# Attention with half-height transposes, in the step order transposes, scores, values

## What is computed

```
s_c = q·kc * scale;      p_c = masked_softmax(s_c)     # compressed keys, 63 of them
s_s = q_rot·k_s * scale; p_s = masked_softmax(s_s)     # selected blocks
s_w = q_rot·k_w * scale; p_w = masked_softmax(s_w)     # window of 512
o = gates[..., 0:1] * (p_c @ vc) + gates[..., 1:2] * (p_s @ v_s) + gates[..., 2:3] * (p_w @ v_w)
```

## Time and profile before

| | |
|---|---|
| median of 3 runs | 2242.99 us (2241.25 to 2245.93) |
| profiled execution | 2246.47 us |
| its span | 2244.4 us |
| TensorE busy | 2174.4 us (97%) |
| VectorE busy | 948.7 us (42%) |
| ScalarE busy | 663.2 us (30%) |
| GpSimd busy | 456.7 us (20%) |
| mean granted TensorE clock | 0.989 |
| the attention loop | from about 181 to 448 us of the span |

### The profile page before, as it was taken

One profiled execution on the slowest core, in us unless ns is written; L12 is line 12 of the kernel. 1 busy time (PEld: TensorE's weight loads), 2 busy tenths in 40 slices (PEclk: granted clock), 3 DMA queues, 4 the chain that ended last, 5 costly groups with the idle time before them and its releaser, 6 DMA issues.

```text
span 2244.4 us, 28818 instructions
## 1 busy us (share of the span) xinstructions
PE 2174.4 (97%) x10100; PEld 1392.4 (62%) x10100; DVE 948.7 (42%) x2027; ACT 663.2 (30%) x1402; POOL 456.7 (20%) x890
## 2 busy tenths in 40 slices
PE   8998999999999999999999999999999999999996
PEld 6454665677678887888885556454544445454542
DVE  0226888764367785354444568411111111111114
ACT  2125666555425561111112220011111111111114
POOL 0002444301100000000000000134343434444340
PEclk9998999999999999999999999999999999999998
DMA  6302000065421111122213123699999999999955
GB/s 210 121 0 104 2 1 1 2 225 218 180 65 32 37 37 40 32 63 75 75 38 127 68 104 117 242 359 338 353 347 340 345 344 349 343 354 332 347 147 228
DMA packets 133213, 378.25 MB, mean 169 GB/s; under 512 B 23891, under 2 KB 81355, under 8 KB 105835
## 3 DMA queue, kind: packets, MB, share of 16 engines
q1 hardware_dynamic: 109587, 292.46, 35.1%
q0 software_dynamic: 23520, 84.36, 13.1%
HBM read 341.48 MB, written 58.00 MB: 178 GB/s over the span
## 4 chain that ended last, share of the span: by engine, by line
PE 87%; DVE 7%; ACT 3%; DMA 2%; issue 1%; SPq 0%; DVEq 0%; POOL 0%; ACTq 0%; POOLq 0%
PE PS L1458 20%; PE PS L1238 19%; PE PS L1469 10%; PE PS L765 9%; PE PS L878 5%; PE PS L1363 5%; PE PS L911 3%; PE PS L948 3%; PE PS L1053 2%; PE PS L813 2%; PE PS L1539 1%; PE PS L1402 1%; PE PS L1185 1%; PE PS L1347 1%; PE PS L1341 1%
## 5 line engine op out<-in xcount | busy, mean ns | idle before, releaser
L1238 PE MATMUL PS<-arena 128*128 128x258 f32 x2352 | 516.1, 382 | 6.3 <-DVE arena L2304 4.7
L1238 PEld LDWEIGHTS PS<-arena 128*128 128x128 f32 x2352 | 446.7, 190 | 73.9 <-DVE arena L2304 5.1
L1549 ACT ACTIVATE arena<-PS 128x512 f32<-128x512 f32 (+9 forms) x602 | 276.8, 471 | 707.3 <-PE PS L765 383.8
L1458 PE MATMUL PS<-arena 128*128 128x512 f32 x1040 | 457.2, 592 | 0.8 <-ACT arena L1549 0.8
L765 PEld LDWEIGHTS PS<-arena 128*128 128x128 f32 (+3 forms) x1950 | 236.6, 158 | 177.7 <-issue 121.4
L1458 PEld LDWEIGHTS PS<-arena 128*128 128x128 f32 x1040 | 192.9, 190 | 218.6 <-issue 217.6
L765 PE MATMUL PS<-arena 128*128 128x128 f32 (+3 forms) x1950 | 284.5, 277 | 25.3 <-DVE arena L2086 7.7
L1469 PE MATMUL PS<-arena 128*128 128x512 f32 x520 | 239.2, 593 | 0.5 <-ACT arena L1549 0.5
L2576 DVE TENSOR_TENSOR arena<-PS,arena 128x256 f32<-128x256 f32 x65 | 27.6, 425 | 432.2 <-ACT arena L1891 425.6
L1469 PEld LDWEIGHTS PS<-arena 128*128 128x128 f32 x520 | 94.0, 191 | 93.9 <-issue 93.3
L2680 POOL MEMSET arena<- 128x2 f32 x1 | 0.1, 100 | 747.4 <-PE PS L1363 747.4
(11 more groups left out here) (338 smaller groups left out, 2215.8 us busy)
## 6 DMA issues: line engine op xcount, KB each, us to landing
arena<-in_w_exp_gate SPq DMA_DIRECT2D x65, 1024.0 KB
arena<-in_w_exp_up SPq DMA_DIRECT2D x65, 1024.0 KB
arena<-in_w_exp_down SPq DMA_DIRECT2D x65, 1024.0 KB
arena<-in_w_in SPq DMA_DIRECT2D x34, 512.0 KB, 4.8
arena<-in_x_prompt SPq DMA_DIRECT2D x16, 512.0 KB, 5.1
expert_rows<-arena SPq DMA_DIRECT2D x16, 512.0 KB
arena<-expert_rows SPq DMA_DIRECT2D x6, 1024.0 KB, 11.0
arena<-in_w_in SPq DMA_DIRECT2D x16, 256.0 KB, 8.0
```

What stands on the lines that cost most here:

```text
L1238: ins = mm(PS[:, bank, 0:QT], lhs[:, l0 + k, :], right[:, r0 + k, c0:c0 + QT], start=first and k == 0, stop=k == kh - 1, skip_group_check= ...
L1458: ins = mm(PS[:, 2 + s, :].rearrange("p (h n) -> p h n", h=2), xgT[:, s, k, :], up_w[w][:, :, k, :], start=k == 0, stop=k == KT - 1)
L1549: return fn(out, in_, ACT.Copy)
```

## The change

`turn_probs` splits every 128x128 transpose into two: query rows 0 to 63 go to bank 4 and rows 64 to 127 to bank 5 (`turn_half`), for both heads, each from 64 partitions with 64 columns of the identity. It now waits for both copies of the unit before at its start. ScalarE copies the first half of the queries of both heads, VectorE the second half (`half_turned`); `PTs` keeps its layout. A compressed unit is copied by ScalarE alone, from both banks. TensorE's order at a place becomes transposes(k-6), scores(k), values(k-7). ScalarE does exps(k-1) and falls(k-1) at place k, after its copy; VectorE does its copy first, then maxima(k) and coefs(k-1). `coefs` leaves the gate out: in tiles 3 to 0 GpSimd's multiplication takes the gate and the reciprocal as its two scalars (the second was the constant 1.0); in tiles 7 to 4 GpSimd makes correction times gate once per group, in a small operation of its own that it waits for, and takes the reciprocal as second scalar. Epsilon moves to a buffer of its own, set in the mixing stage without a semaphore of its own.

```diff
--- before.py
+++ after.py
@@ -261,6 +261,12 @@
                 return kvraw[:, 5:9, P:2 * P].rearrange("p (g t) c -> p g t c", g=2)
             return at(TMP + (5632 if p == 3 else 2816 * half + 1024 * p), 2, u["n"], P)
 
+        def half_turned(k, h):
+
+            n = UNITS[k]["n"]
+            return (PTs[:, k % 2, :, 0:n * P].rearrange("p g (c h q) -> p g c h q", h=2, q=64)[:, :, :, h, :],
+                    PS[:, 4 + h, 0:n * P].rearrange("p (g c q) -> p g c q", g=2, q=64))
+
         def small(slot, off, *shape):
             n = int(np.prod(shape))
             assert off + n <= P
@@ -421,6 +427,7 @@
         widx = rowb[:, 0, 0:2]
         wrow = at(29700, 2)
         st4 = at(29664, 4, 8)
+        eps = at(29708, 1)
 
         met = [sem("pe_met"), sem("act_met"), sem("dve_met")]
 
@@ -765,6 +772,11 @@
                 return nc.tensor.transpose(out, in_, ident[0:n, 0:n])
 
 
+            def turn_half(out, in_, h):
+
+                return nc.tensor.transpose(out, in_[GP[h]], ident[GP[h], 64 * h:64 * h + 64])
+
+
             turned_into = []
 
             def next_bank():
@@ -917,18 +929,17 @@
                 pe.wait_ge(scale_done, k + 1)
                 if k:
                     pe.wait_ge(pt_ev[0], k)
+                if N_PT1[k] > (u["kind"] != "c"):
+                    pe.wait_ge(pt_ev[1], N_PT1[k] - (u["kind"] != "c"))
                 if u["kind"] == "c":
-                    for j in range(4):
-                        src = kvraw[:, 1 + 4 * (u["i"] % 2) + j, 0:P]
-                        ins = turn(PS[:, 4, j * P:(j + 1) * P], src, P)
-                    E.do(ins, pt_done)
+                    src = [kvraw[:, 1 + 4 * (u["i"] % 2) + j, 0:P] for j in range(4)]
                 else:
-                    for g in range(2):
-                        if g and N_PT1[k] > 1:
-                            pe.wait_ge(pt_ev[1], N_PT1[k] - 1)
-                        for c in range(u["n"]):
-                            ins = turn(PS[:, 4 + g, c * P:(c + 1) * P], probs(u)[:, g, c, :], P)
-                        E.do(ins, pt_done)
+                    src = [probs(u)[:, g, c, :] for g in range(2) for c in range(u["n"])]
+                for m, rows in enumerate(src):
+                    for h in range(2):
+                        ins = turn_half(PS[:, 4 + h, m * 64:(m + 1) * 64], rows, h)
+                        if m == len(src) - 1 and (h or u["kind"] != "c"):
+                            E.do(ins, pt_done)
 
             def values(k):
 
@@ -952,16 +963,16 @@
             for k in range(NU + LAG + 1):
                 if k == 2:
                     pe.wait_ge(tokT_ready, 3 * NT - 2)
+                if k == LAG:
+                    pe.wait_ge(tokT_ready, 3 * NT)
+                if 0 <= k - LAG < NU:
+                    turn_probs(k - LAG)
                 if k < NU:
                     scores(k)
                 if k == 0:
                     turn_tile(NT - 1, (2,))
                 if k == 4:
                     turn_tile(NT - 1, (0, 1))
-                if k == LAG:
-                    pe.wait_ge(tokT_ready, 3 * NT)
-                if 0 <= k - LAG < NU:
-                    turn_probs(k - LAG)
                 if 0 <= k - LAG - 1:
                     values(k - LAG - 1)
             E.arrive()
@@ -1655,16 +1666,18 @@
                     act.wait_ge(pt_done, N_PT[k - LAG] - (UNITS[k - LAG]["kind"] != "c"))
                     if k >= LAG + 2:
                         act.wait_ge(pv_done, k - LAG - 1)
-                    w = 512 if UNITS[k - LAG]["kind"] == "c" else UNITS[k - LAG]["n"] * P
-                    E.do(copy(PTs[:, (k - LAG) % 2, 0, 0:w], PS[:, 4, 0:w]), pt_ev[0])
+                    if UNITS[k - LAG]["kind"] == "c":
+                        E.do(copy(PTs[:, (k - LAG) % 2, 0, :].rearrange("p (j h q) -> p h j q", j=4, h=2), PS[:, 4:6, 0:256].rearrange("p h (j q) -> p h j q", j=4)), pt_ev[0])
+                    else:
+                        E.do(copy(*half_turned(k - LAG, 0)), pt_ev[0])
                 if k == 0:
                     tok_T(NT - 1, (2,))
                 if k == 4:
                     tok_T(NT - 1, (0, 1))
-                if k < NU:
-                    exps(k)
-                    if CHUNKED[k]:
-                        falls(k)
+                if 1 <= k <= NU:
+                    exps(k - 1)
+                    if CHUNKED[k - 1]:
+                        falls(k - 1)
             E.arrive()
 
 
@@ -1927,7 +1940,6 @@
                             with act.If(i * 2 + 1 < blocks):
                                 spare(i, 1)
 
-            act.wait_ge(sem("eps_set"), 1)
             for t in range(NT):
                 n = rows_of(t)
                 s, w = st4[0:n, t % 4, :], other[0:n, t, :]
@@ -1936,7 +1948,7 @@
                     act.wait_ge(sem("fin_done"), t - 3)
                 E.step(fn(w.rearrange("p (a b) -> p a b", a=2), PS[0:n, 2 * (t % 4):2 * (t % 4) + 2, :], ACT.Identity, scale=-1.0 / D, accum_out=s[:, 0:1]), sem("totalled"))
                 E.step(fn(w, w, ACT.Square, bias=s[:, 0:1], scale=-float(D), accum_out=s[:, 1:2]))
-                E.do(fn(s[:, 2:3], s[:, 1:2], ACT.Sqrt, bias=st4[0:n, 0, 7:8], scale=1.0 / D), sem("std_done"))
+                E.do(fn(s[:, 2:3], s[:, 1:2], ACT.Sqrt, bias=eps[0:n, :], scale=1.0 / D), sem("std_done"))
 
 
         @block.vector
@@ -2051,19 +2063,15 @@
                     E.do(tt(v, v, g4[:, 0], ALU.mult), coef_done)
                     return
                 h = u["group"] % 2
-                ga = g4[:, 1:3, :, u["j"]]
                 if u["group"] >= 2:
                     dve.wait_ge(scale_done, max(m for m in range(NU) if UNITS[m]["group"] == u["group"] - 2) + 1)
                 if i >= 4:
                     dve.wait_ge(fall_done, REL[k])
                     E.step(tt(part[:, h], fall[:, h], sums[:, h], ALU.mult))
                     E.step(tt(tot[:, h], part[:, h, :, 0, :], part[:, h, :, 1, :], ALU.add))
-                    E.step(V.reciprocal(tot[:, h], tot[:, h]))
-                    E.step(tt(tot[:, h], tot[:, h], ga, ALU.mult))
-                    E.do(tt(coef[:, h], fall[:, h], tot[:, h].unsqueeze(2).broadcast_to([P, 2, 2, 2]), ALU.mult), coef_done)
+                    E.do(V.reciprocal(tot[:, h], tot[:, h]), coef_done)
                 else:
-                    E.step(V.reciprocal(tot[:, h], sums[:, h, :, 0, :]))
-                    E.do(tt(coef[:, h, :, 0, :], tot[:, h], ga, ALU.mult), coef_done)
+                    E.do(V.reciprocal(tot[:, h], sums[:, h, :, 0, :]), coef_done)
 
             def block_out(i):
 
@@ -2071,19 +2079,18 @@
                 E.do(V.tensor_copy(AT[:, :, i * P:(i + 1) * P], PS[:, 6 + i % 2, :].rearrange("p (j q) -> p j q", j=4)), o_ev)
 
             for k in range(NU + LAG + 3):
+                if 0 <= k - LAG < NU and UNITS[k - LAG]["kind"] != "c":
+                    u = UNITS[k - LAG]
+                    dve.wait_ge(pt_done, N_PT[k - LAG])
+                    if k >= LAG + 2:
+                        dve.wait_ge(pv_done, k - LAG - 1)
+                    E.do(V.tensor_copy(*half_turned(k - LAG, 1)), pt_ev[1])
                 if k < NU:
                     maxima(k)
                 if k == 1:
                     rope_queries(NT - 1)
                 if 1 <= k <= NU and (UNITS[k - 1]["kind"] == "c" or UNITS[k - 1]["last"]):
                     coefs(k - 1)
-                if 0 <= k - LAG < NU and UNITS[k - LAG]["kind"] != "c":
-                    u = UNITS[k - LAG]
-                    dve.wait_ge(pt_done, N_PT[k - LAG])
-                    if k >= LAG + 2:
-                        dve.wait_ge(pv_done, k - LAG - 1)
-                    w = u["n"] * P
-                    E.do(V.tensor_copy(PTs[:, (k - LAG) % 2, 1, 0:w], PS[:, 5, 0:w]), pt_ev[1])
                 if 0 <= k - LAG - 2 < NU and (k - LAG - 1 == NU or UNITS[k - LAG - 1]["kind"] == "c"):
                     block_out(UNITS[k - LAG - 2]["i"])
 
@@ -2464,6 +2471,7 @@
                 dve.wait_ge(sem("mix_mm"), m + 1)
                 dve.wait_ge(s_xin[m % 2], 32 + 16 * (m // 2 + 1))
                 if m == 0:
+                    E.do(V.memset(eps[:, :], EPS))
                     dve.wait_ge(sem("mix_ev"), 1)
                     E.step(stt(y, xr[0:n, 0, :], ALPHA, y, ALU.mult, ALU.add), sem("xr_used"))
                 else:
@@ -2606,7 +2614,6 @@
                             with dve.If(i * 2 + 1 < blocks):
                                 spare(i, 1)
 
-            E.do(V.memset(st4[:, 0, 7:8], EPS), sem("eps_set"))
             for t in range(NT):
                 n = rows_of(t)
                 s, y = st4[0:n, t % 4, :], x1tok[0:n, t, :]
@@ -2637,9 +2644,14 @@
                     G.tensor_tensor(pc, pc, coefc[:, u["i"] % 2].unsqueeze(3).broadcast_to([P, 2, 4, 63]), ALU.mult).then_inc(scale_done, 1)
                 else:
                     h, kd = u["group"] % 2, "sw".index(u["kind"])
```

(7 more changed lines are left out.)

## The result

The changed kernel takes 2226.87 us (median of 4 runs, 2226.18 to 2227.41) against 2244.46 for the kernel before on the same chip: 17.6 us less by the medians. The ratio is 0.9916, 95% interval 0.9904 to 0.9928 (the medians alone give 0.9922, which lies inside). Forecast were 23.6. Its profiled span is 2225.1 us, 19.3 less than before.

The account below looks back on a forecast made before the run. TensorE was taken to bound the attention loop. Its saving of 41.3 us less 13, 2.5, 1.4 and 0.8 gives 23.6 us, taken off the median of 2243.0: 2219.4 us, range 2204 to 2234.

Parts of the forecast that it names:

- 13, 2.5 and 0.8: Attention loop losses: 13 us waiting on GpSimd's road, 2.5 VectorE's queue around compressed units, 0.8 exponentials one place later.
- the filling: Start of the attention loop: ScalarE's last token-tile copies also delay unit 3's exponential, charged 1.4 us.
- TensorE's saving: Attention loop: cheaper transposes and dropped change-overs save 38.7 us in ordinary units and 2.6 in compressed ones, together 41.3.
- 0.112 or 0.126: Rival prices per transpose pair: 0.112 us gives 2231.5 (chance 0.08); 0.126, halves one after the other, about 2240 (0.07).
- The change-over: TensorE, transposes to scores: both in 64-row form, so about 0.09 us of a step's fixed part goes.
- The road over GpSimd: Tiles 7 to 4, a group's scores to first transposes: 4.7 us with four chunks, TensorE waiting 0.6 to 1.0 per group.
- GpSimd's second scalar operand is a pointer instead of a constant: 0: GpSimd's multiplications: the pointer costs nothing, else it adds to the road.
- The gate operation with its wait: GpSimd's own gate operation on the road in tiles 7 to 4: adds about 0.3 us.
- VectorE's queue: Tiles 3 to 0: no wait on the road, but VectorE's queue around compressed units costs perhaps 2.5 us.
- The clock: Rival 3, attention loop: pauses bring half-clock lapses, a loss from 14 on; 2253 us, chance 0.05.
- Its other sign: Sign of being wrong: scores waiting for ScalarE in most steps.
- Rival 1: Attention loop: the road is shorter than thought and only VectorE limits; 36 us saved, 2207 us, chance 0.2.

Follow-up runs that it names:

- 7 steps: The changed kernel with one more step (7 instead of 6) between a unit's scores and its transposes: 2215.5 us, ratio 0.9863.
- the halves with the early copy: The kernel before with half-height transposes and VectorE's copy moved to the head of its place, other orders as before: 2234.4 us, ratio 0.9945.
- the changed kernel with a filler: The changed kernel with 16 half transposes of the identity (8 pairs) ahead of TensorE's wait for a group's first multiplication: 2224.3 us, ratio 0.9903.
- halves alone: The kernel before with the half-height transposes and their copies alone, order of all streams and gate as before: 2240.75 us, ratio 0.9971.
- the new orders alone (with the gate moved): The changed kernel with whole transposes and copies by head as before; new order, late exponentials and gate on GpSimd kept: 2252.15 us, ratio 1.0029.

## Why the prediction was right, and where its sizes were off

**The sum by its terms.** Up to its last values matmul the loop became 18.1 us shorter (447.25 to 429.18), where the sum has 23.6. By the windows TensorE's busy time fell by 34.0 us, where 41.3 was forecast; its idle time rose by 15.7, where 13, 2.5 and 0.8 make 16.3; the filling cost 0.3 and not 1.4. So the mechanism and the waits were as forecast, and the term that was sized wrong is TensorE's saving. In the run with 7 steps, whose windows have no lapse, it is 36.8: about 3 us are the lapses, and 4.5 were never there to save. Of these, 0.004 us on each of 560 pairs are 2.2.

**TensorE's new work** was right in kind: 0.067 us for a pair of halves against 0.063 taken, not 0.112 or 0.126, and sixteen halves with three-chunk scores take 1.34 us from 245.91 to 247.25, where the sum has 0.56 + 0.78. The halves do run side by side. The whole transpose's 0.109 doesn't follow as it was worked out, since 1.10 less 0.27 over seven is 0.119; but a group of four takes 0.66 us and one of eight 1.10, and that gives 0.110, so the price stands.

**The change-over**: gone before the scores, as said. But scores and transposes are neighbours in the old order too, so that saving came with the halves, not with the order. The order's use is another, as I read it: VectorE and ScalarE do a step's copies while TensorE computes scores. What is shown is that with any one stream's order put back the gain is smaller or lost (57, 127 and 10 us slower, with 9 to 66 us more at half clock), and that TensorE's order and the late exponentials pay only together (6.5 us on top of the halves with the early copy). The prediction priced the three moves at 0.8 us and some queueing because it only asked what they cost, never what the halves would do without them.

**The road over GpSimd** was the mechanism: one step more took it off and gave 12 us, 13 had been charged. Some 3 of the 12 are the two lapses: the changed kernel with a filler, without a lapse after 201 us, takes 2224.3, and 7 steps are 9 us faster than that; TensorE's idle time fell by 8.6. Idle TensorE on the multiplications is 20.2 us, of which 2.6 stand before the first group, which the forecast left to the filling: 17.6 against 16.2 forecast. The step that failed there is "GpSimd's second scalar operand is a pointer instead of a constant: 0": it costs 76 ns each, two on every road. The gate operation with its wait is 0.31 us, as taken. Put together, the move of the gate left the road as long as it was.

**Tiles 7 to 4** gave 11.6 us where 41.3 - 13.5 - 13 - 0.8 makes 14.0: busy time fell by 24.1 of 27.8, and idle time rose by 12.5 of 13.8. **Tiles 3 to 0** gave 6.8 where 13.5 - 2.5 makes 11. The 2.5 us for VectorE's queue were about right. Take tile 3 above, and tiles 2 to 0 from the run with 8 pairs of filler, which issues none there and has no lapse: busy time fell by 4.1 and 7.2, so by 11.3 of 13.5; idle time rose by 1.1 and 1.9, so by 3.0; the lapse took another 1.6. The loop ends at 429 and not near 424, with VectorE busy for 86% of it.

**The clock** was set down as a rival that needs 14 lapses for a loss. The mechanism is real, in small: two lapses in the changed kernel. Without a lapse the last window takes 44.5 us (7 steps, whose tile 3 is unchanged) or 45.0 (8 pairs of filler) instead of 46.6, so one costs 1.6 to 2.1 us. They belong to what the forecast lacks, and were not in its sum: a granted clock of 1.00 from 199 us on did not come true, and the clock at half inside the loop, which it named as a sign of being wrong, did occur, for 7 of 227 us. Its other sign did not: scores waited for ScalarE nine times in 104 steps.

**Rival 1**, no road and only VectorE's floor, said 2207. It did not happen, and even 7 steps, with VectorE busy for 35.0 of 37.7 us in tile 7, come to 2215.5.

## What to carry to other kernels

When one engine's work in a pipeline written out by hand gets shorter, list for each stream what stands first at a step and what it waits for: here halves alone gave 6 us, the new orders alone (with the gate moved) lost 6, both together gave 19. And test moves in pairs: two of them did nothing or harm by themselves and paid together. Work out the longest road between two uses of the shortened engine as well as its sum; if a road over other engines binds, one more step of lag takes it off: 9 to 12 us here, where moving one of its parts to another engine gave nothing. And look at the granted clock in each window before explaining a difference between two variants by their waits.

## What the runs showed of the hardware

Pauses of TensorE of 1.6 to 2 us, once in about 10 us of otherwise dense work, went with five lapses to 1.2 GHz of 3.4 us each in tiles 7 to 4, and transposes of the identity in those pauses removed all five and 9 us of time. One such lapse cost 1.6 to 2.1 us in the loop's last window. Transposes of 64 rows in both halves of the array overlap, at 0.067 us a pair against 0.109 for a whole one. A GpSimd multiplication by two per-row scalars takes 76 to 79 ns longer than by one and a constant, at three chunks and at four.
